# New start addresses in SBUF for the stationary stage buffers (hT, mT) and the moving ones (oT, yT) of a two-block transformer kernel

## The reference, cut to what matters

```python
def swiglu(x, w_gate, w_up, w_down):                 # D_FF = 2816, used in ffn0 and ffn1
    return (jax.nn.silu(x @ w_gate) * (x @ w_up)) @ w_down
...
    h = x @ w_in                                     # hybrid_mixer of the first block
...
    merged = (gates[:, :, 0] * (merge_heads(o_m) @ w_br_moba) + ...)
    return merged @ w_out
...
        mixed = (g_a * (ya @ w_a2d[i]) + g_b * (yb @ w_b2d[i])) @ w_o[i]   # second block
...
        f = (jax.nn.gelu(f_gate) * f_val) @ w_down[i]                      # ffn2
```

## Time and profile before

| | |
|---|---|
| time, median of 3 runs | 1125.13 us (1124.93 to 1125.46) |
| span of the profiled execution, first to last instruction | 1122.6 us |
| PE matmul busy | 1094.1 us (97%), 8110 instructions |
| PE load of stationary operands busy | 1023.2 us (91%), 8110 instructions |
| POOL busy | 902.3 us (80%) |
| ACT busy / DVE busy | 621.2 us (55%) / 495.1 us (44%) |
| mean granted clock of TensorE | 0.998 |

### The profile page before, as it was taken

One profiled execution on the slowest core, in us unless ns is written; L12 is line 12 of the kernel. 1 busy time (PEld: TensorE's weight loads), 2 busy tenths in 40 slices (PEclk: granted clock), 3 DMA queues, 4 the chain that ended last, 5 costly groups with the idle time before them and its releaser, 6 DMA issues.

```text
span 1122.6 us, 22288 instructions
## 1 busy us (share of the span) xinstructions
PE 1094.1 (97%) x8110; PEld 1023.2 (91%) x8110; DVE 495.1 (44%) x904; ACT 621.2 (55%) x1002; POOL 902.3 (80%) x695
## 2 busy tenths in 40 slices
PE   8999999999999999999999999999999999999997
PEld 7999998999998998999999899889999798999985
DVE  4422113202456554421126655774766256454463
ACT  4444444654667866544443775555666565555564
POOL 6999996898664596999999589577355898999985
PEclk9999999999999999999999999999999999999999
DMA  7866665666342454766665466335233565666652
GB/s 244 282 204 193 187 195 165 206 222 192 115 131 78 130 184 139 230 202 198 192 182 181 135 193 188 118 116 159 65 94 127 183 202 172 180 197 187 189 184 77
DMA packets 52774, 191.29 MB, mean 170 GB/s; under 512 B 5856, under 2 KB 6112, under 8 KB 52320
## 3 DMA queue, kind: packets, MB, share of 16 engines
q1 hardware_dynamic: 50688, 182.47, 52.6%
q10 hardware_dynamic: 2016, 7.81, 2.1%
HBM read 189.21 MB, written 1.05 MB: 169 GB/s over the span
## 4 chain that ended last, share of the span: by engine, by line
POOL 51%; issue 27%; PE 19%; ACT 1%; POOLq 1%; DVE 1%; DMA 1%; SPq 0%; DVEq 0%; ACTq 0%
POOL weights_low L533 51%; PE banks L575 10%; PE acc L575 8%; DMA ring<-in_stream 1%; POOLq L539 0%; ACT weights_high L1440 0%; POOLq L530 0%; ACT tmp L1686 0%; ACT tmp L1956 0%; PE acc L749 0%; PE banks L766 0%; DVE act_buf L2016 0%; DVE res L2162 0%; POOL stat L547 0%; DVE xs L2174 0%
## 5 line engine op out<-in xcount | busy, mean ns | idle before, releaser
L533 POOL TENSOR_TENSOR weights_low<-ring,weights_high 128x512 fp32r<-128x512 f32 x686 | 899.2, 1345 | 208.7 <-ACT weights_high L1440 206.5
L1440 ACT CAST weights_high<-ring 128x1024 fp32r<-128x1024 f32 x343 | 356.1, 1047 | 216.4 <-PE banks L575 132.0
L575 PE MATMUL banks<-xT_high,weights_high 128*128 128x256 f32 x1264 | 351.5, 278 | 1.2 <-POOL weights_low L533 1.1
L575 PE MATMUL banks<-xT_low,weights_high 128*128 128x256 f32 x1264 | 350.3, 277 | 0.0
L575 PE MATMUL banks<-xT_high,weights_low 128*128 128x256 f32 x1264 | 350.3, 277 | 0.0
L575 PEld LDWEIGHTS banks<-xT_high,weights_high 128*128 128x128 f32 x1264 | 237.4, 188 | 4.2 <-issue 1.5
L575 PEld LDWEIGHTS banks<-xT_low,weights_high 128*128 128x128 f32 x1264 | 237.7, 188 | 2.3
L575 PEld LDWEIGHTS banks<-xT_high,weights_low 128*128 128x128 f32 x1264 | 237.9, 188 | 0.0
L1991 DVE TENSOR_TENSOR hf<-act_buf,banks 128x256 f32<-128x256 f32 x40 | 16.8, 421 | 225.2 <-ACT act_buf L1466 211.0
L575 PE MATMUL acc<-xT_high,weights_high 128*128 128x256 f32 x408 | 108.8, 287 | 1.8 <-ACT xT_high L1539 1.0
L575 PE MATMUL acc<-weights_high,hT_high 128*128 128x512 f32 x264 | 104.0, 394 | 2.2 <-issue 1.6
(11 more groups left out here) (362 smaller groups left out, 1577.5 us busy)
## 6 DMA issues: line engine op xcount, KB each, us to landing
ring<-in_stream SPq DMA_DIRECT2D x343, 512.0 KB, 3.7
rows<-in_big_rows ACTq DMA_DIRECT2D x3, 1024.0 KB, 8.2
rows<-in_big_rows ACTq DMA_DIRECT2D x3, 512.0 KB, 4.0
cst<-in_consts ACTq DMA_DIRECT2D x3, 470.5 KB, 4.8
xs<-in_x_tm ACTq DMA_DIRECT2D x2, 512.0 KB, 7.3
out<-xs SPq DMA_DIRECT2D x4, 256.0 KB, 2.1
gates<-in_x_fm SPq DMA_DIRECT2D x2, 256.0 KB, 4.2
ring<-in_stream SPq DMA_DIRECT2D x2, 256.0 KB, 4.3
```

The source lines that it names most:

```text
L533: last = nc.gpsimd.tensor_tensor(wlo[:, slot, hs], ring[:, slot, hs], whi[:, slot, hs].bitcast(F32), ALU.subtract)
L575: ins = nc.tensor.matmul(o, lhsT, rhs, start=start, stop=stop, **kw)
L1440: nc.scalar.copy(whi[:, ch % RING, :], ring[:, ch % RING, :]).then_inc(S["hi_ready"], 1)
```

## The change

No instruction is added, removed or moved: the lists of the instructions of all engines are the same in the same order. What changes is where buffers begin. The filler in front of `xT` (352 bytes) is replaced by four small buffers that are needed anyway (`stat`, `nmx2`, `den2`, `coef2`, together 352 bytes), so `xT` stays where it was; `tmp` moves up behind it; the filler in front of the stage buffers shrinks, and two new fillers of 896 bytes stand in front of `oT_low` with its neighbours and of `yT`.

```diff
         res = sb("res", [2, D])
-        sb("fill_x", [88])
-        xT = pair("xT", [KD, T])
         stat = sb("stat", [64])
-        sb("fill_scalars", [12])
-        tmp = sb("tmp", [2, 2 * T])
-
         nmx2 = sb("nmx2", [2, 4])
         den2 = sb("den2", [2, 4])
         coef2 = sb("coef2", [2, 4])
-        sb("fill_stage", [144])
+        xT = pair("xT", [KD, T])
+        tmp = sb("tmp", [2, 2 * T])
+        sb("fill_stage", [32])
         hT = pair("hT", [GROUP, T], in_ffn)
...
         wT_sb = sb("wT_sb", [4, 384], block_one)
+        sb("fill_o", [224], block_one)
...
+        sb("fill_y", [224], block_two)
         yT = pair("yT", [8, T], block_two)
-        sb("pad3", [3 * 8 * P + 4 * 512 - 16 * T], block_two)
+        sb("pad3", [3 * 8 * P + 4 * 512 - 16 * T - 224], block_two)
```

## The result

The changed kernel takes 1129.23 us (median of 22 runs), the kernel before beside it 1124.84 us (22 runs). The ratio is 1.0036, with an interval from 1.003 to 1.0043: slower by 0.36%, beyond the 0.2% that a measurement of this kernel can tell. Two executions of the changed kernel and one of the kernel before were disturbed (1205.57, 2198.69 and 1348.17 us) and are left out of the ratio. The forecast was 1119.7 us and the range ended at 1128, so the time came out on the other side of no change and 1.2 us above the range.

What follows compares the result with a forecast made beforehand. PE was taken as the bound, through distances between matmuls. Gains of 3.2 us (hT), 0.9 (mT, pE) and 1.3 (oT, yT) sum to 5.4 us, taking 1125.1 to 1119.7 us; range 1112 to 1128 us.

Steps and rivals of the forecast that it cites:

- What bounds the kernel: Whole kernel: PE, busy in every microsecond of the FFNs, sets the pace; a tile may quicken 0.40 us before POOL binds.
- Feature-major matmuls of xT: xT moving, 48 matmuls in each of 66 FFN tiles: addresses stay, so 5.47 us a tile stays; no change taken.
- the worse rhythm: xT moving past weights, 256 columns: matmuls 117.8 ns apart, as behind z, in place of 113.3 ns in FFN tiles.
- slower, the worse rhythm in the FFNs: FFN tiles: new hT leaves xT's matmuls at 117.8 ns, 0.18 us a tile, 66 tiles 11.9 us; 1131.6 us; chance 0.17.
- hT, 32 to 192: FFN rows with hT stationary, 792 matmuls: 4.1 ns less each, like xT stationary in z at 229.2 ns; 3.2 us gained.
- the prediction's signs of being wrong: In an FFN tile: xT's 48 matmuls take 5.65 us, or hT's distance stays at 233 ns.
- no change: Large products: z's 4.1 ns advantage comes from something other than the start address; time stays 1125.1 us; chance 0.15.
- mT and pE: Products with mT and pE stationary, 32 to 192, 216 matmuls: 4.0 ns less each, 0.9 us gained.
- oT and yT: Branch products with oT and yT moving, 32 to 64, 408 matmuls: 3.1 ns less each at 114.0 ns, 1.3 us gained.
- The rule that was weighed: TensorE's two independent SBUF read ports: addresses would not matter and time would stay 1125.1 us; the forecast set it aside.
- Lockstep: hT and mT 64 bytes behind the moving weights: 226.7 ns for 512 columns, 1116.8 us in all; chance 0.22.

Runs made afterwards that it cites:

- the moving ones alone: Changed kernel with hT, mT and pE back at 32, oT and yT left at 64: 1124.89 us, ratio 0.9995 to the kernel before.
- a shift: Short extra matmul ahead of tiles: changed kernel, tiles 17, 19, 21 of each FFN, 1129.43 us; hT at 128, every tile from the third on, 1136.03 us.
- all at 64 and the extra matmul: Changed kernel with hT, mT, pE, oT, yT at 64 like xT, plus an 8-column matmul ahead of tile 4 in each FFN: 1125.03 us, ratio 1.0.

## Why the prediction was wrong

**What bounds the kernel: right.** PE sets the pace, and what is put on the distances goes into the time. POOL's waits followed.

**Feature-major matmuls of xT: the step that failed.** "I take no change and keep both for the rivals" cost the forecast its sign. Of 54 tiles 27 fell into the worse rhythm, about 4.6 us. The rival "slower, the worse rhythm in the FFNs" had the mechanism and the price of a tile (0.18 us; measured 0.19) and wanted all 66 tiles or at least 30; but the first four of each FFN run as one row of 192, and 54 stand behind hT. It was half of these, which neither the forecast nor the rival had seen, because a tile's rhythm sets the phase of the next: in the trace of the changed kernel a last hT distance of 229 to 230 ns stands ahead of each of the 27 long ones and one of 233 to 236 ahead of each of the 27 short ones. That distance is a mark of the phase, not a rule: before the change, 229 to 231 ns stand ahead of all 54 tiles, and all are short. The point from which that rival decides, 30 tiles, was worked out against a gain of 5.4 us, of which less than half came.

**hT, 32 to 192: wrong in its price.** The nearest row, xT stationary at 64, was chosen because both starts are multiples of 64. That hT stays at 233 ns was one of the prediction's signs of being wrong, and it is what the rival "no change" said of hT. 192 gives 232 to 233 ns and 64 gives 229 (320 with hT too, but 233.3 with mT). Of the 3.2 us, 0.1 came (183.4 to 183.3 us above). All rows with hT together are 0.7 us shorter (185.8 to 185.2), but 0.5 of that lie in five distances above 300 ns at the beginning and the end of an FFN (2.4 us before, 1.9 after).

**mT and pE: wrong by the same step.** Of 0.9 us nothing came; mT is at 233.2 ns as before.

**oT and yT: right in size, with some luck.** 1.3 us were forecast, with 1.6 if all come at 113.3 ns; distances that are under 300 ns before and after fell by 0.8 and 0.6, 1.4 us, and 24 matmuls with oT take 2.72 us where 2.74 was expected. With the moving ones alone the loss is gone and this gain remains, though 1.3 us is less than a comparison can tell. The luck is that the rows of that execution took the better rhythm, which the start of 64 does not secure: the row of 198 with oT took 24.22 us before and 23.64 after, but 24.13 and 24.15 us in the runs with hT at 96 and 320, where oT lies at 64 as well.

**The rule that was weighed.** The Trainium skill, "TensorE: Matmul & The Clock Gate", "Step-by-step: what each phase is for", says that a load takes no read bandwidth from the running matmul. Taken alone, that speaks against an effect of any address, and these runs do not bear that out. With xT, oT, yT and the weights left in place, the start of the stationary operand, and of the stage buffers that move with it, took the distance at 512 columns from 226.7 to 233.2 ns, and that of the following xT matmuls from 113.3 to 117.9. Whatever the mechanism is, these numbers do not fit a time that is free of where the operands lie.

**Lockstep: refuted for 192.** A stationary operand 64 bytes behind the moving one gives 232 to 233 ns, not 226.7. The 226.7 ns exist, at equal starts.

**What stays open.** What the rhythm is physically; why the phase turns over from tile to tile at 192 and 0, and not at 32 or 96; why a shift turns a tile at 192 and not at 128; whether hT itself or a buffer that moves with it sets xT's rhythm. The runs show that addresses count, and so does what a row meets as it begins, not by what circuit.

## What to carry to other kernels

Where matmuls run in unbroken rows, take distances from start to start over a whole row: here they differ by up to 6% at the same recorded length. A new start address is worth what the whole stage makes of it, the rows behind it too, and its price can't be taken over from another address that merely shares a divisor. Run such a layout in several executions before trusting a gain below 0.5%, since one program can hold two rhythms.

## What the runs showed of the hardware that was not expected

- The start of one operand, with the stage buffers behind it, changes the rhythm of matmuls that do not read it: moving hT from 32 to 96 takes xT's 48 from 5.47 to 5.66 us.
- Equal starts gave the shortest distance at 512 columns (226.7 ns) and the longest at 256 (120 ns).
- A row can change its rhythm behind a short wait, where the prediction said that it stays in it: with mT at 320, 69 matmuls at 233.3 ns, then 22 at 229.1.
- A whole FFN can hold the long rhythm in one execution and not in another of the same program (18 tiles at 5.65 us, or at 5.47). Layouts with all tiles long spread least: 0.25 us over 4 runs at 96 and 0.66 over 5 with all at 128, against 7.5 us over 12 with all at 64 and the extra matmul.
